# Five row buffers instead of seven from row 168 on, two kept tiles of the odd mixer's output weights

## The reference

```python
def short_conv_mixer(xn, w_in, conv_w, w_out):
    bg, cg, hx = jnp.split(xn @ w_in, 3, axis=-1)      # w_in 1024 x 3072
    u = cg * hx
    y = causal_conv_of_width_3(u, conv_w)
    return (bg * y) @ w_out                            # w_out 1024 x 1024

def peer(xn, w_q, sub_keys, u, v):
    q = xn @ w_q                      # 8 heads, two half keys of 128 each
    # per token and head: the 16 best of 128 x 128 experts, by the sum of two half scores
    # gate = softmax over the 16
    hid = gelu(dot(xn, u[expert]))    # for each of 8 x 16 experts of each token
    return sum(gate * hid * v[expert])
```

## Time and profile before

| | us |
|---|---|
| three runs | 2147.6, 2150.67, 2150.3; median 2150.3 |
| the profiled execution's own time | 2149.94 |
| its span in the profile | 2148.1 |

### The profile page before, as it was taken

One profiled execution on the slowest core, in us unless ns is written; L12 is line 12 of the kernel. 1 busy time (PEld: TensorE's weight loads), 2 busy tenths in 40 slices (PEclk: granted clock), 3 DMA queues, 4 the chain that ended last, 5 costly groups with the idle time before them and its releaser, 6 DMA issues.

```text
span 2148.1 us, 20313 instructions
## 1 busy us (share of the span) xinstructions
PE 1849.5 (86%) x5992; PEld 871.0 (41%) x5992; DVE 1285.7 (60%) x3071; ACT 714.7 (33%) x2002; POOL 663.4 (31%) x593
## 2 busy tenths in 40 slices
PE   9999999997899999999868887677888867888876
PEld 4445555332245445454423333323433433334322
DVE  1333433221122768666478797987777888777765
ACT  1232221111111346344334333433333343444442
POOL 2121001110000334334334353454334345444432
PEclk9999999999999999999999999899999999999998
DMA  7432366999796999999999999999999999999996
GB/s 247 168 119 77 144 247 254 409 418 419 324 357 242 378 421 393 421 416 421 421 422 421 420 411 421 407 401 421 421 421 421 420 411 415 421 421 420 415 421 283
DMA packets 114801, 779.40 MB, mean 363 GB/s; under 512 B 16048, under 2 KB 17760, under 8 KB 21632
## 3 DMA queue, kind: packets, MB, share of 16 engines
q0 software_dynamic: 78928, 542.37, 61.4%
q1 hardware_dynamic: 32256, 225.65, 26.3%
q10 hardware_dynamic: 3504, 10.04, 1.2%
HBM read 780.10 MB, written 10.49 MB: 368 GB/s over the span
## 4 chain that ended last, share of the span: by engine, by line
DMA 32%; DVE 17%; issue 9%; PE 8%; POOL 5%; ACT 2%; DVEq 0%; POOLq 0%; ACTq 0%
DMA arena<-in_c_rows_dram,arena 32%; DVE arena L2732 8%; POOL arena L2829 5%; PE banks L2718 3%; PE banks L1824 2%; DVE x L2738 2%; PE banks L369 1%; DVE arena L2637 1%; DVE arena L2628 1%; PE banks L1915 1%; DVE arena L2631 1%; ACT arena L2795 1%; DVE arena L2673 1%; DVE arena L2666 1%; DVE arena L2670 1%
## 5 line engine op out<-in xcount | busy, mean ns | idle before, releaser
L2718 PE MATMUL banks<-arena 128*128 128x512 f32 x1784 | 892.2, 630 | 225.9 <-ACT arena L2795 222.4
L2829 POOL DMA_INDIRECT arena<-in_c_rows_dram,arena x512 | 585.8, 1144 | 839.9 <-PE banks L2718 481.8
L2732 DVE CUSTOM_DVE_ANT_0 arena<-arena,xn 128x1024 f32<-128x1024 f32 x512 | 625.8, 1223 | 302.0 <-DMA arena<-in_c_rows_dram,arena 296.8
L2718 PEld LDWEIGHTS banks<-arena 128*128 128x128 f32 x1784 | 320.6, 195 | 684.0 <-ACT arena L2795 414.9
L2786 ACT ACTIVATE small<-small 128x1 f32<-128x1 f32 x512 | 103.5, 202 | 732.7 <-DVE small L2732 728.7
L314 PE MATMUL banks<-ring,hT 128*128 128x512 f32 (+1 forms) x480 | 202.1, 577 | 0.0
L2795 ACT ACTIVATE arena<-ident,small 128x128 f32<-128x128 f32 x446 | 179.1, 401 | 42.0 <-ACT small L2789 1.5
L376 ACT COPY arena<-banks 128x512 f32<-128x512 f32 (+4 forms) x218 | 101.0, 492 | 254.9 <-PE banks L360 107.4
L2789 ACT ACTIVATE small<-small 128x1 f32<-128x1 f32 x512 | 150.8, 295 | 49.0 <-DVE arena L2644 0.4
L314 PEld LDWEIGHTS banks<-ring,hT 128*128 128x128 f32 x480 | 87.9, 191 | 100.2 <-issue 98.4
L402 POOL TENSOR_TENSOR small<-small 128x1 f32<-128x1 f32 (+4 forms) x24 | 33.4, 1391 | 285.1 <-DVE small L398 266.0
(11 more groups left out here) (319 smaller groups left out, 1799.9 us busy)
## 6 DMA issues: line engine op xcount, KB each, us to landing
arena<-in_c_experts_dram SPq DMA_DIRECT2D x51, 1024.0 KB, 20.1
ring<-in_c_w_in_dram SPq DMA_DIRECT2D x30, 1024.0 KB
ring<-in_c_experts_dram SPq DMA_DIRECT2D x30, 1024.0 KB
ring<-in_c_w_q_dram SPq DMA_DIRECT2D x18, 1024.0 KB
ring<-in_c_odd_w_in_dram SPq DMA_DIRECT2D x15, 1024.0 KB
ring<-in_c_even_w_in_dram SPq DMA_DIRECT2D x12, 1024.0 KB
arena<-in_c_even_w_in_dram SPq DMA_DIRECT2D x10, 1024.0 KB, 17.3
arena<-in_c_rows_dram,arena POOLq DMA_INDIRECT x512
```

The costliest lines, as they stand in the source:

```text
L2718: r = e.matmul(banks[:, bank_of[("acc", L, c, hf)], :], diag[:, diag_of[m], :], rows[:, row_of[m], D + hf * 512:D + (hf + 1) * 512], start ...
L2732: e.tensor_tensor_reduce(u, u, xn[:, c, :], 1.0, 0.0, ALU.mult, ALU.add, hid3[:, c, h, k:k + 1]).then_inc(ve.sem, ve.up(("u", p)))
L2829: e.indirect_dma_start(rows[:, b, :], None, table_uv, bass.IndirectOffsetOnAxis(ap=eix[:, c, 16 * h + k:16 * h + k + 1], axis=0)).then_inc ...
```

## The change

From row 168 on, places 4 and 6 leave the round of row buffers, so that five are left (0, 1, 2, 3, 5). They keep the two tiles of the second half of `oddout`'s columns, and both chunks use them: in chunk 0 they are loaded there, once the last row in each place is used up (row 167 for place 4, row 165 for place 6), and in chunk 1 they are not loaded. Six `oddout` loads are left of eight, and the ring of three slots has four tiles fewer to turn over.

```diff
+FEWER = 168
+GIVEN_UP = (4, 6)
...
+        KEPT_OUT = {(1, 0): NSLOT + 4, (1, 4): NSLOT + 6}
+
+        def out_tile(c, hf, k):
+            return ("oddout", "both", hf, k) if (hf, k) in KEPT_OUT else ("oddout", c, hf, k)
...
                     if what[0] == "out" and what[3] % 4 == 0:
                         _, c, hf, k = what
-                        load(e, ("oddout", c, hf, k), w_odd_out[2 * hf + k // 4])
+                        kept = KEPT_OUT.get((hf, k))
+                        if kept is not None and c == 0:
+                            m_ = given_up[kept - NSLOT]
+                            s = ve if on_dve(m_) else pe
+                            e.wait_ge(s.sem, s.at(("v", m_)))
+                        if kept is None or c == 0:
+                            load(e, out_tile(c, hf, k), w_odd_out[2 * hf + k // 4], kept)
...
-                name, w = ("oddres", c, hf), ("oddout", c, hf, k - k % 4)
+                name, w = ("oddres", c, hf), out_tile(c, hf, k - k % 4)
...
         free, last_in, row_of, row_before = [0, 1, 2, 5, 6, 3, 4], {}, [], []
         for m in range(LAST):
+            if m == FEWER:
+                given_up = {b: last_in[b] for b in GIVEN_UP}
+                free = [b for b in free if b not in GIVEN_UP]
             b = free.pop(0)
             free.append(b)
```

## The result

The changed kernel takes 2218.1 us (median of four runs, 2212.5 to 2223.45), the kernel before 2150.49 beside it: 1.0324 times as long, with a 95% interval of 1.031 to 1.0337. That is 68 us slower, where I forecast 9 slower and a range that ended at 17. The direction was right, the size was off by a factor of eight.

What follows compares the result with a forecast made beforehand. DMA engines at 421 GB/s were taken as the bound, with row buffers keeping them going; from 2149.9 us, -5.0 + 7.7 + 2.5 + 3.5 = +8.7 gave 2158.6, as median 2159.0, range 2150.5 to 2167.

Steps and rivals of the forecast that it cites:

- The bound: From the 18th slice on, DMA engines full at 421 GB/s, 2.49 us a row; two loads fewer save 5.0 us.
- The three terms: Ask 0.95 us, ask's end to first bytes 1.8, row's transfer 2.49: 5.2 needed of 7.8, so last 128 rows cost nothing.
- The budget's form: Quiet row held 4.38 us, ask starts 0.28 later; of five buffers' 12.44 us, 7.78 remain from ask to landing.
- The three places: Rows 222, 239 and 251, behind late asks, land 1.8, 2.8 and 3.1 us late, together 7.7 us.
- Small shortages: Where long holds meet a late DVE, positions 175 to 195, around 295, 330, 370: 2.5 us, bounds 0 and about 8.
- The norms: At four norms behind row 168 POOL's root waits behind an ask, delaying DVE's scaling 2.1 us: 3.5 us, bounds 0 and 8.4.
- The moved loads: SP waits at place 4's tile until row 167 is used up, 1214.1 us; tiles behind it not needed yet: no cost.
- The rivals: Buffers hold, 2145.3 us (0.08); a draw, 2149 to 2153 (0.20); norms and small places at upper bounds, 2164 to 2169 (0.12).
- the upper bounds: Rival 3: small places cost 8 us and norms 8.4, +19 in all, 2164 to 2169 us; chance 0.12.
- what would show it: Signs: six `oddout` loads, row 384 some 8 us later, dips near 1355, 1400, 1430, last 128 rows still 2.49 us apart.

Runs made afterwards that it cites:

- the curve: Four kernels' extra time in rows 384 to 508 by quiet-row time from ask to landing: 7.8 us 16.8, 8.1 us 13.1, 9.3 us 0.5, 10.2 us -1.0.
- the run with `AHEAD = 3`: Changed kernel with POOL's asks three rows ahead of the position in its order instead of five: 2214.74 us, ratio 1.03.
- the run with the saving undone: Changed kernel, five buffers from row 168 on, but all eight output-weight tiles loaded through the ring as before: 2214.33 us, ratio 1.0314.
- five buffers in the tail: Kernel before with five buffers only from row 384 on and no kept tiles: 2163.25 us, ratio 1.0065.
- the diagonal's asks: Kernel before, seven buffers, but from row 384 on the ask for row m also waits for row m - 5's diagonal matrix: 2149.36 us, ratio 1.0.

## Why the prediction was wrong, step by step

- **The bound** was read rightly: 421 GB/s, and 2.49 us a row. With seven buffers two tiles less are worth 4.5 us (forecast 5.0).
- **The step that failed: "Need 0.95 + 1.8 + 2.49 = 5.2 of 7.8 us: in gathers alone five buffers do, with 2.5 us to spare. The last 128 rows should cost nothing."** They cost 21 us, 15 to 17 with nothing else changed. The three terms were right at row 451, and their sum is the landing of the first of 16 engines (5.05 there). The term that was missing is the time from the first engine's landing to the last one's. Ten rows between 390 and 508 have a first share within 5.3 us of the ask: in eight of them the last came after 7.3 to 8.5 us, in two after 5.4 and 6.3. And the step of the curve lies between 8.1 and 9.3. I had read the start of the engines and never the end of the last. The evidence was in the trace of before: within one row the first and the last engine's landings lay 5.4 us apart in the median, and I wrote that the engine furthest behind "still has work" without asking what it would do with less to go on.
- **The budget's form held**: hold + ask + landing = number of buffers x 2.49 us. With 8.2 in place of 5.2 a row may be held 12.44 - 0.28 - 8.2 = 4.0 us. Quiet rows are held 4.38. Quiet rows get through with 7.8 us, as I read it because their engines don't run dry, but there is no reserve anywhere: a row whose buffer comes 1 to 1.5 us late (for 116 of the 216 rows between 168 and 383 the next ask came over 5.2 us after the read) finds most of them dry and pays, and nothing brings that back. In the middle 48 of 197 landings came over 1 us later than 2.49 us behind the one before, mostly by up to 2.5.
- **The three places** (7.7 us): the rows forecast to be late are late, but by less. In the changed kernel rows 222, 239 and 251 land 0.4, 0.9 and 1.4 us later than 2.49 us behind the row before (forecast 1.8, 2.8 and 3.1). Only with the neighbours, rows 222 to 226, 239 and 240, 251 and 252, does it come to 7.3 us, and that the sum agrees is luck: rows 234, 245 and 256, which I hadn't named, are late by 1.7, 2.4 and 1.5. The mechanism was right here; I took the exceptions for the whole.
- **Small shortages** (2.5 us, at most 8): this term should have carried some 60 us. It was bounded by counting places at which 5.2 us are not to be had, so it inherited the error.
- **The norms** (3.5, at most 8.4): the root does stand behind the ask. Before position 205 of the changed kernel, the ask, the root and the scaling that waits for it:

```profile
1326.01 0.95 POOL L2844 DMA_INDIRECT arena<-in_c_rows_dram,arena  x1 [2.61 <-PE banks L2730]
1326.98 0.57 POOL L404 TENSOR_TENSOR small<-small 128x1 f32<-128x1 f32 x1
...
1327.66 1.41 DVE L419 SCALAR_TENSOR_TENSOR xn<-x,small,gain 128x512 f32<-128x512 f32 x2 [2.61 <-POOL small L404]
```

  DVE waits 2.6 us there (I had 2.1) and 10.3 in all four, but in the run with `AHEAD = 3`, where these waits are gone, its waits for landings are 4.2 us longer, so a part of them only took the place of a landing's.
- **The moved loads** (0): nothing speaks against it, though the run with the saving undone settles it only to some 7 us. SP's lines around the wait for row 167; the two tiles for the given-up places go out together, 83 us ahead of the changed kernel's first product that needs them (1293.2):

```profile
1182.85 0.90 SPq L277 DMA_DIRECT2D ring<-in_c_odd_w_out_dram  x2
1210.10 0.80 SPq L277 DMA_DIRECT2D arena<-in_c_odd_w_out_dram  x2
```

- **The rivals**: I gave the upper bounds 0.12 and stopped at 19 us, because each bound was built on the same 5.2. The sentence under "what would show it", that slower last rows mean the time from ask to landing is over 7.8 us, named the failure before it happened. A rival with that price (7.8 short by 0.4 at every long hold, in all 343 rows) was missing.

## What to carry to other kernels

A buffer's round has to cover hold, ask and the landing of the last engine's share; read that last number at a row whose engines ran dry, not from the start of the transfer, and not from the average rate. While there is reserve, a buffer is worth little (seven to six: 4.6 us between rows 168 and 384, nothing in the total), and the next one can cost 3% (six to five), so test the count on both sides of the step before spending a place. A total that doesn't move may be two changes that cancel: hold the stretches of the trace against each other, the program's end too. Where a buffer has to go, shorten the longest holds first: the v halves moved from DVE to PE were worth some 25 us with five buffers, 5 with six and 3 with seven.

## What the runs showed of the hardware that was not expected

- A row that finds most of its 16 engines dry lands 5.4 to 8.5 us after its ask; eight of ten such rows between 390 and 508 of the changed kernel took over 7 us. The first engine's share comes at 4.9 to 5.3 us, the rest straggle. The Trainium skill, "DMA: Bandwidth & Descriptors", section "Anatomy of one DMA — SWDGE (gpsimd) path", has a fit of 2.0 us and the bytes at 436 GB/s for one DMA, an estimate of 4.4 us here. The trace doesn't agree: the quickest row behind row 384 in the changed kernel took 5.38, and most of those ten 1.7 to 1.9 times the fit.
- Packets of 8 KB get slower when the engines run short. Between rows 384 and 508 the kernel before has 36 of 15,970 that took over 0.6 us (median 0.31), the changed one 340 of 15,872, five buffers in the tail 305, six buffers 35, the diagonal's asks 73. The mean rises from 314.5 to 329.0 ns, which is 15,872 x 14.5 ns / 16 = 14 us for each engine, beside the 21 lost there; how much of it fell on the engine that landed last is not shown. Half of the slow ones start right behind the end of an engine's share of a row (of all packets 16% do; of the 36 slow ones before, 16). So the first packet of a share seems to be the one that is slow; that was only read from the traces, not tested.
- The gather's ask took 0.95 us in most cases and up to 2.0 in others, in both kernels; the plain one 0.53 to 0.58.
- POOL's drain at the end of the program takes 7.55 us in the six kernels with seven buffers and 2.08 or 2.33 in the thirteen with fewer. What it depends on was not tested.
